# Cross attention with scores three steps in front, another order of VectorE's and ScalarE's work in a step, and the first scores inside the projection of V

## The chip, the cores and the metric

The kernel runs on one core of a Trainium2 chip. The metric is the device time of one execution in microseconds (us). Lower is better.

TensorE (PE in the profile) multiplies matrices and transposes; PEld is its loading of stationary operands. VectorE is DVE, ScalarE is ACT, GpSimd is POOL, and SyncE (SP) issues the loads of weights. Every engine works through its own list of instructions in order, and semaphores tie the lists together.

## The reference

Two transformer blocks on one sequence of 1024 tokens with width 1024. The change touches the cross attention of the first block alone: four heads of width 256 over a memory of 256 rows.

```
    xq = (rmsnorm(h, norm_x_g[l]) @ w_xq[l]).reshape(B, S, XATT_HEADS, XATT_HEAD_DIM)
    mn = rmsnorm(mem, norm_mem_g[l])
    xk = (mn @ w_xk[l]).reshape(B, M, XATT_HEADS, XATT_HEAD_DIM)
    xv = (mn @ w_xv[l]).reshape(B, M, XATT_HEADS, XATT_HEAD_DIM)
    sc = jnp.einsum('bshd,bmhd->bhsm', xq, xk).astype(jnp.float32) * (XATT_HEAD_DIM ** -0.5)
    pr = jax.nn.softmax(sc, axis=-1).astype(xv.dtype)
    xo = jnp.einsum('bhsm,bmhd->bshd', pr, xv).reshape(B, S, D_MODEL)
    h = h + xo @ w_xo[l]
```

## The kernel before

**Precision.** Every fp32 operand of a product is held as two parts, hi (rounded) and lo (the rest), and a product is three matmuls: hi by hi, hi by lo, lo by hi. ScalarE or GpSimd makes the hi part, and the lo part is a subtraction on VectorE or GpSimd.

**The stages around the change.** They follow each other in the lists of all engines, written out by hand:

1. Projection of K, eight jobs. SyncE loads a block of 512 KB into one of two slots of `raw`. GpSimd's `split` runs a tiny instruction (L524) and then makes `w_hi` (L525). VectorE's `memory_lo` makes `w_lo` (L2040), which also lets SyncE load the slot anew. TensorE multiplies (L657). ScalarE copies the result to `KTH` and VectorE subtracts to get `KTL` (L2053), which frees the PSUM slot.
2. Projection of V, eight blocks k. The same pipeline of weights, but all blocks are summed in the two PSUM slots `PJ[0]` and `PJ[1]` (L870). In between VectorE makes the lo parts of the queries with `query_low` (L2048), `B_lo` from `XQ` and `B_hi`, both in SBUF. In the end ScalarE makes `XVH` (L1404) and VectorE `XVL` (L2060), which frees the two slots.
3. The attention: 16 steps i, each for 128 tokens and two heads. In a step TensorE computes the scores (`x_score`, 12 matmuls, L888). VectorE takes the maxima of the two heads and scales them (`x_maximum`, L2065 and L2068). ScalarE takes the exponentials with their sums (`x_exp`, L1412). VectorE inverts the sums and scales the probabilities `XP` (`x_norm`, L2072 and L2074). TensorE transposes them (`x_turn`, L897). ScalarE copies the result to `XPT_hi` (`x_copy`, L1421), and VectorE subtracts to get `XPT_lo` (`x_split`, L2080). After four steps the transposed probabilities of 512 tokens are complete, and from then on each step also has one product with V (`x_values`, 6 matmuls, L909). ScalarE copies its result to `B_hi` (`x_out`, L1426), and VectorE subtracts to get `B_lo` (L2085).
4. The output projection, whose first job takes four of its eight blocks between the last value products (L657), and then the rest.

Before the change TensorE's iteration i is score(i+2), values(i-5), turn(i). VectorE's is out(i-6), split(i-1), maximum(i+2), norm(i+1). ScalarE's is out(i-6), copy(i-1), exp(i+2). All of `x_score(2)` and later waits for both PSUM slots to be free after the projection of V. A value product n waits for the `B_lo` of product n-2, since two PSUM banks take turns.

## Time and profile before

| what | value |
|---|---|
| median of three runs | 2959.33 us (2959.02 to 2960.76) |
| the profiled execution's own time | 2960.54 us |
| its span, first to last instruction | 2958.5 us |
| mean granted TensorE clock | 0.997 |
| TensorE matmuls busy | 2893.2 us, 98% of the span |
| VectorE busy | 1896.5 us, 64% |
| ScalarE busy | 1031.2 us, 35% |
| GpSimd busy | 1278.3 us, 43% |

The stages above lie between 570 and 707 us of the span. The shares are means over the whole kernel. The cross attention is under 4% of it, and TensorE's share there has to be read from its own stretch.

### The profile page before, as it was taken

How to read it: one execution, taken by the hardware profiler on the slowest of the kernel's cores; microseconds unless marked ns; L12 is line 12 of the kernel's file. 1: busy time of each engine (PE TensorE's matmuls, PEld its weight loads, DVE VectorE, ACT ScalarE, POOL GpSimd, SP SyncE). 2: the span in 40 equal slices, each digit the busy share in tenths (PEclk: the TensorE clock that was granted, in tenths of full speed). 3: DMA queues.
4: the chain of work that ended last, by engine and by line, in shares of the span. 5: the costliest groups of instructions: out<-in, count | busy, mean ns of one | idle time of the engine just before them, and what ended most of it. 6: DMA issues, size and time to landing. Idle time of an engine off the chain costs nothing.

```text
span 2958.5 us, 37245 instructions
## 1 busy us (share of the span) xinstructions
PE 2893.2 (98%) x14048; PEld 2336.6 (79%) x14048; DVE 1896.5 (64%) x1849; ACT 1031.2 (35%) x1411; POOL 1278.3 (43%) x1043
## 2 busy tenths in 40 slices
PE   9999999978999999999999999999999999999998
PEld 7887778867878888888777777888688778888886
DVE  7998764465575787776565656221675856778764
ACT  4116751133343332223253435112732533233321
POOL 0003323331364677763333332332433646777760
PEclk9999999999999999999999999999999999999999
DMA  3131021220132423232212121421431224232231
GB/s 143 50 74 49 2 97 46 78 79 21 36 110 100 154 94 108 98 107 86 114 61 79 60 76 59 163 105 50 181 142 46 86 97 143 98 123 100 100 114 57
DMA packets 77840, 265.29 MB, mean 90 GB/s; under 512 B 7552, under 2 KB 8064, under 8 KB 74368
## 3 DMA queue, kind: packets, MB, share of 16 engines
q1 hardware_dynamic: 57552, 183.89, 18.5%
q10 hardware_dynamic: 20144, 79.44, 7.4%
q8 instruction: 95, 1.56, 0.2%
q14 instruction: 49, 0.40, 0.0%
HBM read 208.25 MB, written 52.95 MB: 88 GB/s over the span
## 4 chain that ended last, share of the span: by engine, by line
PE 78%; DVE 11%; ACT 5%; DMA 4%; issue 2%; POOL 1%; ACTq 0%; DVEq 0%; SPq 0%; POOLq 0%
PE psum L657 50%; PE psum L947 15%; PE psum L1161 3%; DMA hid<-TT 2%; PE psum L1046 2%; PE psum L762 1%; DMA raw<-weights 1%; PE psum L778 1%; PE psum L792 1%; DVE WSX L2107 1%; ACT TT L1508 1%; DVE SX L2107 1%; DVE TT L2151 1%; PE psum L1112 1%; PE psum L1099 1%
## 5 line engine op out<-in xcount | busy, mean ns | idle before, releaser
L657 PE MATMUL psum<-A_hi,w_hi 128*128 128x512 f32 x1536 | 478.8, 393 | 1.7 <-POOL w_lo L536 0.5
L524 POOL TENSOR_TENSOR small<-par 128x1 f32<-128x1 f32 x149 | 42.3, 284 | 997.8 <-PE psum L657 844.0
L657 PE MATMUL psum<-A_lo,w_hi 128*128 128x512 f32 x1536 | 473.3, 389 | 0.0
L657 PE MATMUL psum<-A_hi,w_lo 128*128 128x512 f32 x1536 | 472.9, 389 | 0.0
L657 PEld LDWEIGHTS psum<-A_hi,w_hi 128*128 128x128 f32 x1536 | 287.0, 188 | 68.4 <-issue 6.9
L657 PEld LDWEIGHTS psum<-A_hi,w_lo 128*128 128x128 f32 x1536 | 288.3, 188 | 60.3
L657 PEld LDWEIGHTS psum<-A_lo,w_hi 128*128 128x128 f32 x1536 | 288.3, 188 | 60.2
L530 POOL TENSOR_TENSOR w_lo<-raw,w_hi 128x1024 fp32r<-128x1024 f32 (+1 forms) x133 | 331.0, 2488 | 11.1
L657 PE MATMUL psum<-B_hi,w_hi 128*128 128x512 f32 x832 | 257.5, 391 | 1.1 <-DVE B_lo L2319 1.1
L657 PE MATMUL psum<-B_hi,w_lo 128*128 128x512 f32 x832 | 256.1, 389 | 0.0
L657 PE MATMUL psum<-B_lo,w_hi 128*128 128x512 f32 x768 | 236.5, 389 | 0.0
L947 PE MATMUL psum<-XS,w_hi 128*128 128x512 f32 x768 | 236.3, 389 | 0.0
L947 PE MATMUL psum<-XS,W 128*128 128x512 f32 x864 | 211.8, 389 | 1.0 <-POOL w_lo L608 1.0
L947 PEld LDWEIGHTS psum<-XS,W 128*128 128x128 f32 x864 | 161.9, 188 | 35.6 <-POOL w_lo L608 2.2
L548 POOL TENSOR_SCALAR P<-P,small 128x704 f32<-128x704 f32 x64 | 54.5, 864 | 313.1 <-DVE small L1914 313.1
L657 PEld LDWEIGHTS psum<-B_hi,w_hi 128*128 128x128 f32 x832 | 156.0, 188 | 34.6 <-DVE B_lo L2319 1.5
L657 PEld LDWEIGHTS psum<-B_hi,w_lo 128*128 128x128 f32 x832 | 156.2, 188 | 32.5
L657 PEld LDWEIGHTS psum<-B_lo,w_hi 128*128 128x128 f32 x768 | 144.2, 188 | 30.0
L947 PEld LDWEIGHTS psum<-XS,w_hi 128*128 128x128 f32 x768 | 144.2, 188 | 29.8
L1463 ACT ACTIVATE XS<-XSF 128x1024 fp32r<-128x1024 f32 x84 | 89.3, 1063 | 223.7 <-DMA XSF<-hid 107.3
L998 PE MATMUL psum<-SX,WX_hi 128*128 128x512 f32 x512 | 158.3, 390 | 6.9 <-DVE SX L2107 6.9
L525 POOL TENSOR_SCALAR w_hi<-raw 128x1024 fp32r<-128x1024 f32 (+1 forms) x149 | 155.2, 1042 | 0.0
(361 smaller groups left out, 5522.2 us busy)
## 6 DMA issues: line engine op xcount, KB each, us to landing
raw<-weights SPq DMA_DIRECT2D x256, 512.0 KB, 3.3
hid<-TT ACTq DMA_DIRECT2D x60, 512.0 KB, 2.7
XSF<-hid SPq DMA_DIRECT2D x48, 512.0 KB, 5.3
BM<-rel_bias ACTq DMA_DIRECT2D x8, 1152.0 KB, 7.9
gate_spill<-RU SPq DMA_DIRECT2D x16, 512.0 KB, 3.0
ULF<-hid SPq DMA_DIRECT2D x6, 1024.0 KB, 7.0
x_spill<-H ACTq DMA_DIRECT2D x1, 4096.0 KB, 12.1
R<-gate_spill ACTq DMA_DIRECT2D x8, 512.0 KB, 4.6
```

The costliest lines, as they stand in the source:

```text
L524: pool.tensor_tensor(small[:, 12:13], par[:, 0:1], par[:, 0:1], ALU.mult)
L525: hi = pool.tensor_scalar(w_hi[:, s, 0:kb], raw[:, s, 0:kb], 1.0, 1.0, ALU.mult, ALU.mult)
L530: pool.tensor_tensor(w_lo[:, s, 0:kb], raw[:, s, 0:kb], f32(w_hi[:, s, 0:kb]), ALU.subtract).then_inc(S["w_split"], 1)
L548: pool.tensor_scalar(probs, probs, rsums[p % 3][:, h:h + 1], 1.0, ALU.mult, ALU.mult).then_inc(S["probs"], 1)
L657: last = pe.matmul(PJ[s][:, c:c + step], w[:, s, k, :], b[:, k, c:c + step], start=(k == 0 and i == 0), stop=(k == kblocks - 1 and i == 2))
L762: last = pe.matmul(pair_bank(p, h)[:, at_key:at_key + n], Q[rows, m, query:query + P], moving, start=True, stop=True)
L947: last = pe.matmul(bank, w[a][:, at_w + i, :], XS[layer][:, x, b, i, :], start=(i == 0 and t == 0), stop=(i == 1 and t == 2))
L998: last = pe.matmul(bank, WX[a][:, slot, k, :], moving[b][:, k, :], start=(k == 0 and i == 0), stop=(k == 3 and i == 2))
L1046: last = pe.matmul(PX[:, 1024 * g + HALF * h:1024 * g + HALF * h + HALF], WG[slot][:, 2 * d + g, :], RU[:, HALF * h:HALF * h + HALF], star ...
L1161: last = pe.matmul(fin_bank(n), w, x[:, k, half_of(h)], start=(k == 0 and i == 0), stop=(k == KB - 1 and i == 2))
L1463: tallies["st_hi"](act.activation(x[:, i, 0], xf[:, i, 1], ACT.Copy))
L2107: tally(dve.tensor_tensor(out, a, b, ALU.subtract))
```

## The change

It has five parts, all in the cross attention. No matmul, no load and no ScalarE instruction is added or removed.

- Scores 0 and 1 are computed inside the projection of V, behind its blocks 3 and 4. In the loop the score runs three steps in front, not two. The score banks are assigned so that step 2 needs only `PJ[0]` and step 4 only `PJ[1]`.
- TensorE's iteration becomes score(i+3), turn(i), values(i-5). The four early blocks of the output projection come one iteration earlier, and the last two value products follow each other.
- VectorE's iteration becomes maximum(i+3), norm(i+1), split(i-1), out(i-6). ScalarE's becomes copy(i-1), out(i-6), exp(i+3).
- The two scalings of the maxima (two instructions of one column) become one of two columns.
- The eight `query_low` are spread over the projections of K and V, at most one between two `memory_lo`. ScalarE's `XVH` of the first slot no longer waits for the second slot's last matmuls, and maxima, exponentials and norms of steps 0 and 1 stand in front of `XVL`.

```diff
         def x_bank(i):
-            at_col = 3072 + HALF * i if i < 2 else HALF * (i % 4)
+            at_col = 3072 + HALF * i if i < 2 else HALF * ((i - 2) % 4)
...
             def x_score(i):
                 pair, t = i // TT, i % TT
-                if i == 2:
-                    for s in range(2):
-                        pe.wait_ge(free[s], ROUNDS["xo"])
+                if i % TT == 0:
+                    pe.wait_ge(S["x_lo"], 4 * pair + 4)
+                if i in (2, 4):
+                    pe.wait_ge(free[i // 2 - 1], ROUNDS["xo"])
...
+            for k in range(KB):
+                q, s = ROUNDS["xv"] + k // 2, k % 2
+                wait_split(pe, q, s, "memory")
+                for r in range(2):
+                    if k == 0:
+                        pe.wait_ge(free[r], q)
...
+                    if k == KB - 1 and r == 0:
+                        last.then_inc(S["xv_half"], 1)
+                last.then_inc(S["products"], 1)
+                if k in (3, 4):
+                    x_score(k - 3)
...
-            x_score(0)
-            x_score(1)
-            for i in range(X_STEPS + X_BEHIND):
-                if i + 2 < X_STEPS:
-                    x_score(i + 2)
+            x_turn(0)
+            x_score(2)
+            x_turn(1)
+            x_score(3)
+            x_score(4)
+            for i in range(2, X_STEPS + X_BEHIND):
+                if i + 3 < X_STEPS:
+                    x_score(i + 3)
+                if i < X_STEPS:
+                    x_turn(i)
                 if i >= X_BEHIND:
                     x_values(i - X_BEHIND)
-                if i < X_STEPS:
-                    x_turn(i)
-                elif i < X_STEPS + 4:
-                    job(ROUNDS["xo"], 0, B, order=[i - X_STEPS], ready=outputs_ready)
+                if X_STEPS - 1 <= i < X_STEPS + 3:
+                    if i == X_STEPS - 1:
+                        pe.wait_ge(S["x_exp"], 2 * X_STEPS)
+                    job(ROUNDS["xo"], 0, B, order=[i - X_STEPS + 1], ready=outputs_ready)
...
             x_exp(0)
             x_exp(1)
-            for i in range(X_STEPS + X_BEHIND + 1):
+            act.wait_ge(S["xv_half"], 1)
+            tallies["m_hi"](act.activation(XVH[:, 0, :], PJ[0], ACT.Copy))
+            wait_job(act, ROUNDS["xv"] + 3, 1)
+            tallies["m_hi"](act.activation(XVH[:, 1, :], PJ[1], ACT.Copy))
+            x_copy(0)
+            x_exp(2)
+            x_copy(1)
+            x_exp(3)
+            x_exp(4)
+            for i in range(2, X_STEPS + X_BEHIND + 1):
+                if 2 < i <= X_STEPS:
+                    x_copy(i - 1)
                 if i > X_BEHIND:
                     x_out(i - X_BEHIND - 1)
-                if 1 <= i <= X_STEPS:
-                    x_copy(i - 1)
-                if i + 2 < X_STEPS:
-                    x_exp(i + 2)
+                if i + 3 < X_STEPS:
+                    x_exp(i + 3)
...
-                for block in {8: (0, 1), 9: (2, 3), 10: (4,), 11: (5,), 12: (6,), 13: (7,)}.get(n, ()):
-                    query_low(block)
+                if n in (1, 3, 5, 7, 8, 9, 10, 11):
+                    query_low(n // 2 if n < 8 else n - 4)
+                if n in (12, 13):
+                    x_maximum(n - 12)
+            x_norm(0)
+            x_norm(1)
             for r in range(2):
                 dve.wait_ge(S["m_hi"], 18 + r)
                 dve.tensor_tensor(XVL[:, r, :], PJ[r], f32(XVH[:, r, :]), ALU.subtract).then_inc(free[r], 4)
...
-                for e in range(2):
-                    done = tl["x_max"] if e else chain
-                    done(dve.tensor_scalar(lowest[e][i % 3], mx[:, e:e + 1], -X_DH ** -0.5, None, ALU.mult))
+                tl["x_max"](dve.tensor_scalar(lowest_of[i % 3], mx, -X_DH ** -0.5, None, ALU.mult))
...
-            for i in range(X_STEPS + X_BEHIND + 1):
-                if i > X_BEHIND:
-                    x_out(i - X_BEHIND - 1)
-                if 1 <= i <= X_STEPS:
-                    x_split(i - 1)
-                if i + 2 < X_STEPS:
-                    x_maximum(i + 2)
-                if i + 1 < X_STEPS:
-                    x_norm(i + 1)
+            x_split(0)
+            x_maximum(2)
+            x_split(1)
+            x_maximum(3)
+            x_norm(2)
+            x_maximum(4)
+            for i in range(2, X_STEPS + X_BEHIND + 1):
+                if i + 3 < X_STEPS:
+                    x_maximum(i + 3)
+                if 2 <= i < X_STEPS - 1:
+                    x_norm(i + 1)
+                if 2 < i <= X_STEPS:
+                    x_split(i - 1)
+                if i > X_BEHIND:
+                    x_out(i - X_BEHIND - 1)
```

The same three moves as the built programs have them. First VectorE in the projection of V, before the change: `w_lo` is `memory_lo`, `B_lo` is `query_low`, two of them behind one `w_lo` at first.

```order
458 L2040 TENSOR_TENSOR w_lo<-raw,w_hi 128x1024 x2
459 L2048 TENSOR_TENSOR B_lo<-XQ,B_hi 128x1024 x2
460 L2040 TENSOR_TENSOR w_lo<-raw,w_hi 128x1024
461 L2048 TENSOR_TENSOR B_lo<-XQ,B_hi 128x1024 x2
462 L2040 TENSOR_TENSOR w_lo<-raw,w_hi 128x1024
463 L2048 TENSOR_TENSOR B_lo<-XQ,B_hi 128x1024
```

The same engine after the change, from the last blocks of the projection of V to `XVL` and the first `split`.

```order
470 L2085 TENSOR_TENSOR B_lo<-XQ,B_hi 128x1024
471 L2054 TENSOR_TENSOR w_lo<-raw,w_hi 128x1024
472 L2062 TENSOR_REDUCE small<-psum 128x2
473 L2063 TENSOR_SCALAR small<-small 128x2
474 L2054 TENSOR_TENSOR w_lo<-raw,w_hi 128x1024
475 L2062 TENSOR_REDUCE small<-psum 128x2
476 L2063 TENSOR_SCALAR small<-small 128x2
477 L2067 RECIPROCAL small<-small 128x2
478 L2069 TENSOR_TENSOR XP_105<-XP_105,small 128x512
479 L2067 RECIPROCAL small<-small 128x2
480 L2069 TENSOR_TENSOR XP_106<-XP_106,small 128x512
481 L2101 TENSOR_TENSOR XVL<-psum,XVH 128x1024 x2
```

The maxima of steps 0 and 1 moved in between and behind the last `w_lo`, and two norms now stand in front of the two `XVL`, for which scores 2 and 4 wait.

Next, one iteration of VectorE in the middle of the attention, before the change (XP_105 to XP_108 are the four buffers of probabilities, the first B_lo and XPT_lo are out and split).

```order
512 L2085 TENSOR_TENSOR B_lo<-psum,B_hi 128x512
513 L2080 TENSOR_TENSOR XPT_lo_112<-psum,XPT_hi_110 128x4x128
514 L2065 TENSOR_REDUCE small<-psum 128x2
515 L2068 TENSOR_SCALAR small<-small 128x1 x2
516 L2072 RECIPROCAL small<-small 128x2
517 L2074 TENSOR_TENSOR XP_105<-XP_105,small 128x512
```

And after it.

```order
517 L2062 TENSOR_REDUCE small<-psum 128x2
518 L2063 TENSOR_SCALAR small<-small 128x2
519 L2067 RECIPROCAL small<-small 128x2
520 L2069 TENSOR_TENSOR XP_105<-XP_105,small 128x512
521 L2075 TENSOR_TENSOR XPT_lo_112<-psum,XPT_hi_110 128x4x128
522 L2080 TENSOR_TENSOR B_lo<-psum,B_hi 128x512
```

The maximum went from behind out and split to their front, and lost one of its two scalings.

Last, ScalarE in the middle of the attention before the change: exp (XP), out (B_hi), copy (XPT_hi).

```order
321 L1412 ACTIVATE XP_106,small<-psum,small 128x256 x2
322 L1426 ACTIVATE B_hi<-psum 128x512
323 L1421 ACTIVATE XPT_hi_110<-psum 128x4x128
324 L1412 ACTIVATE XP_107,small<-psum,small 128x256 x2
325 L1426 ACTIVATE B_hi<-psum 128x512
```

And after it.

```order
320 L1417 ACTIVATE XP_106,small<-psum,small 128x256 x2
321 L1426 ACTIVATE XPT_hi_110<-psum 128x4x128
322 L1431 ACTIVATE B_hi<-psum 128x512
323 L1417 ACTIVATE XP_107,small<-psum,small 128x256 x2
324 L1426 ACTIVATE XPT_hi_109<-psum 128x4x128
```

Copy and out changed places, and the exponentials between them are those of a step one further in front.

## Rows read from the trace of the kernel before

**Rows 1.** The waits from 595 to 707 us: us in total, times, longest.

```profile
PE psum L897 <- DVE XP L2074: 14.7, 14, 2.7
PE psum L870 <- DVE w_lo L2040: 4.4, 5, 1.5
```

**Rows 2.** Stretches: length, PE, PEld, DVE, ACT, POOL busy, granted clock, DMA share, GB/s.

```profile
632.00:635.00 3.00, 3.00 (x17) 3.00 (x17) 1.80 (x6) 1.73 (x5) 0.00 (x0) 0.57 0.00 0
...
660.00:683.00 23.00, 17.72 (x111) 14.35 (x110) 16.68 (x36) 11.65 (x30) 0.00 (x0) 1.00 0.00 1
```

**Rows 3.** TensorE in order of time: start, us, instruction, idle before it.

```profile
595.53 0.70 PE L870 MATMUL psum<-w_hi,MH 128*128 128x512 f32 x2 [1.09 <-DVE KTL L2053]
...
605.65 0.74 PE L870 MATMUL psum<-w_hi,MH 128*128 128x512 f32 x2 [1.52 <-DVE w_lo L2040]
...
613.57 0.72 PE L870 MATMUL psum<-w_hi,MH 128*128 128x512 f32 x2 [0.37 <-DVE w_lo L2040]
...
620.63 0.73 PE L870 MATMUL psum<-w_hi,MH 128*128 128x512 f32 x2 [0.52 <-DVE w_lo L2040]
...
627.40 0.36 PE L888 MATMUL psum<-KTH,B_hi 128*128 128x256 f32 x1 [0.89 <-DVE XVL L2060]
...
631.81 1.11 PE L897 MATMUL psum<-ident,XP 128*128 128x128 f32 x4 [2.74 <-DVE XP L2074]
...
647.46 0.40 PE L909 MATMUL psum<-XPT_hi,XVH 128*128 128x512 f32 x1
...
682.55 0.50 PE L909 MATMUL psum<-XPT_hi,XVH 128*128 128x512 f32 x1 [0.39 <-DVE XPT_lo L2080]
...
706.98 0.62 PE L657 MATMUL psum<-B_hi,w_hi 128*128 128x512 f32 x2
```

**Rows 4.** TensorE in one step: turn, first score, first value matmul.

```profile
657.58 0.66 PE L897 MATMUL psum<-ident,XP 128*128 128x128 f32 x4 [1.03 <-DVE XP L2074]
658.00 0.36 PE L888 MATMUL psum<-KTH,B_hi 128*128 128x256 f32 x1
...
659.50 0.40 PE L909 MATMUL psum<-XPT_hi,XVH 128*128 128x512 f32 x1
```

**Rows 5.** VectorE in the same step.

```profile
658.58 0.69 DVE L2085 TENSOR_TENSOR B_lo<-psum,B_hi 128x512 fp32r<-128x512 f32 x1 [1.05 <-ACT B_hi L1426]
659.30 0.69 DVE L2080 TENSOR_TENSOR XPT_lo<-psum,XPT_hi 128x512 fp32r<-128x512 f32 x1
660.03 0.69 DVE L2065 TENSOR_REDUCE small<-psum 128x2 f32<-128x512 f32 x1
660.76 0.34 DVE L2068 TENSOR_SCALAR small<-small 128x1 f32<-128x1 f32 x2
661.13 0.17 DVE L2072 RECIPROCAL small<-small 128x2 f32<-128x2 f32 x1
661.33 0.69 DVE L2074 TENSOR_TENSOR XP<-XP,small 128x512 f32<-128x512 f32 x1
```

**Rows 6.** ScalarE from one step's exponentials to the next.

```profile
656.68 0.47 ACT L1412 ACTIVATE XP<-psum,small 128x256 f32<-128x256 f32 x1 [2.07 <-DVE small L2068]
...
657.88 0.60 ACT L1426 ACTIVATE B_hi<-psum 128x512 fp32r<-128x512 f32 x1
...
661.18 0.47 ACT L1412 ACTIVATE XP<-psum,small 128x256 f32<-128x256 f32 x1 [2.08 <-DVE small L2068]
```

**Rows 7.** VectorE and GpSimd side by side in the projection of V and behind it.

```profile
600.98 3.36 DVE L2048 TENSOR_TENSOR B_lo<-XQ,B_hi 128x1024 fp32r<-128x1024 f32 x2
602.22 1.05 POOL L525 TENSOR_SCALAR w_hi<-raw 128x1024 fp32r<-128x1024 f32 x1
...
622.86 2.41 POOL L530 TENSOR_TENSOR w_lo<-raw,w_hi 128x1024 fp32r<-128x1024 f32 x1
624.90 2.36 DVE L2060 TENSOR_TENSOR XVL<-psum,XVH 128x1024 fp32r<-128x1024 f32 x2 [3.19 <-ACT XVH L1404]
```

More of the change, by code:

```diff
@@ L195, in build @@
         sums = [small[:, 82 + 2 * i:84 + 2 * i] for i in range(3)]
+        lowest_of = [small[:, 76 + 2 * i:78 + 2 * i] for i in range(3)]
         rsums = [small[:, 88 + 2 * i:90 + 2 * i] for i in range(3)]
@@ L859, in _ @@
             rounds("xk", 4, (MH, ML), width=N_MEM)
-            for k in range(KB):
-                q, s = ROUNDS["xv"] + k // 2, k % 2
-                wait_split(pe, q, s, "memory")
-                if k == 0:
-                    for slot in range(2):
-                        pe.wait_ge(free[slot], q)
-                for r in range(2):
-                    for a, b in ((MH, w_hi), (ML, w_hi), (MH, w_lo)):
-                        wide = b[:, s].rearrange("p a b -> p (a b)")
-                        for c in range(2):
-                            last = pe.matmul(PJ[r][:, HALF * c:HALF * c + HALF], a[:, k, P * r:P * r + P],
-                                             wide[:, HALF * c:HALF * c + HALF],
-                                             start=(k == 0 and b is w_hi and a is MH), stop=(k == KB - 1 and b is w_lo))
-                last.then_inc(S["products"], 1)
-            split_by[0] = "late"
             def x_score(i):
                 pair, t = i // TT, i % TT
-                if i == 2:
-                    for s in range(2):
-                        pe.wait_ge(free[s], ROUNDS["xo"])
+                if i % TT == 0:
+                    pe.wait_ge(S["x_lo"], 4 * pair + 4)
+                if i in (2, 4):
+                    pe.wait_ge(free[i // 2 - 1], ROUNDS["xo"])
                 if i >= 6:
@@ L890, in x_score @@
                 last.then_inc(S["x_scores"], 1)
+            for k in range(KB):
[4 more added lines that the diff above has]
+                        pe.wait_ge(free[r], q)
+                    for a, b in ((MH, w_hi), (ML, w_hi), (MH, w_lo)):
+                        wide = b[:, s].rearrange("p a b -> p (a b)")
+                        for c in range(2):
+                            last = pe.matmul(PJ[r][:, HALF * c:HALF * c + HALF], a[:, k, P * r:P * r + P],
+                                             wide[:, HALF * c:HALF * c + HALF],
+                                             start=(k == 0 and b is w_hi and a is MH), stop=(k == KB - 1 and b is w_lo))
+                    if k == KB - 1 and r == 0:
[3 more added lines that the diff above has]
+                    x_score(k - 3)
+            split_by[0] = "late"
             def x_turn(i):
@@ L911, in x_values @@
                 last.then_inc(S["x_pv"], 1)
[L913 to L918 removed]
+            outputs_ready = (S["x_lo"], [KB + 8 * (k // 4) + 5 + k % 4 for k in range(KB)])
+            x_turn(0)
[8 more added lines that the diff above has]
+                    x_turn(i)
                 if i >= X_BEHIND:
                     x_values(i - X_BEHIND)
[L921 to L924 removed]
+                if X_STEPS - 1 <= i < X_STEPS + 3:
+                    if i == X_STEPS - 1:
+                        pe.wait_ge(S["x_exp"], 2 * X_STEPS)
+                    job(ROUNDS["xo"], 0, B, order=[i - X_STEPS + 1], ready=outputs_ready)
             job(ROUNDS["xo"], 0, B, order=[4, 5, 6, 7], ready=outputs_ready)
@@ L1401, in _ @@
                 tallies["m_hi"](act.activation(B_hi[:, n, :], XQ[:, n, :], ACT.Copy))
-            wait_job(act, ROUNDS["xv"] + 3, 1)
-            for r in range(2):
-                tallies["m_hi"](act.activation(XVH[:, r, :], PJ[r], ACT.Copy))
             def x_exp(i):
@@ L2044, in _ @@
                 memory_lo(ROUNDS["xk"], s)
-            def query_low(n):
-                dve.wait_ge(S["m_hi"], 2 * n + 3)
-                chain(dve.tensor_tensor(B_lo[:, n, :], XQ[:, n, :], f32(B_hi[:, n, :]), ALU.subtract))
-            for n in range(2 * KB):
-                if n < KB:
-                    dve.wait_ge(S["m_hi"], 2 * n + 2)
-                    dve.tensor_tensor(KTL[:, n, :], PJ[n % 2][:, 0:N_MEM], f32(KTH[:, n, :]), ALU.subtract).then_inc(free[n % 2], 1)
-                if n + 2 < 2 * KB:
-                    memory_lo(ROUNDS["xk"] + 1 + n // 2, n % 2)
-                for block in {8: (0, 1), 9: (2, 3), 10: (4,), 11: (5,), 12: (6,), 13: (7,)}.get(n, ()):
-                    query_low(block)
-            for r in range(2):
-                dve.wait_ge(S["m_hi"], 18 + r)
-                dve.tensor_tensor(XVL[:, r, :], PJ[r], f32(XVH[:, r, :]), ALU.subtract).then_inc(free[r], 4)
             def x_maximum(i):
```

19 lines of the change are left out of this document (14 added, 5 removed).

## The prediction

> **What bounds the kernel now.** I read the page first: TensorE's matmuls are busy 98% of the span, so a gain can only come where TensorE waits. Next I read who waited for whom from 595 to 707 us [rows 1]. TensorE's transposes waited 14.7 us, in 14 places, for VectorE's scaling of the probabilities. Its blocks in the projection of V waited 4.4 us for the lo parts of the weights. So this stretch is not bound by TensorE. Third, the stretch from 660 to 683 us, steps of the middle [rows 2]: TensorE is busy 17.72 of 23 us, VectorE 16.68, and the clock is fully granted. No engine is full, which is the mark of a ring: engines that hand one step's work around and wait for each other.
>
> The ring can be read from one step. ScalarE starts the exponentials at 656.68 and again at 661.18, 4.50 us later [rows 6]. They take 1.20 (656.68 to 657.88), and out copies 0.60 more [rows 6]. VectorE, after a hop of 0.1, does out and split (658.58 to 660.03, 1.45) and then the maximum with two scalings (660.03 to 661.10, 1.07) [rows 5], and a hop of 0.08 later the next exponentials begin. 1.20 + 0.60 + 0.10 + 1.45 + 1.07 + 0.08 = 4.50. The maximum stands behind out and split, which stand behind ScalarE's out, which stands behind the previous exponentials. TensorE is not in the ring. Its step is 0.42 of turn, 1.50 of scores [rows 4] and some 1.40 of values (six matmuls at 0.23), 3.32 together, so it idles 1.2 us in every 4.5.
>
> **The steady steps.** The change puts the maximum in front, so it waits only for a score made long ago. Following the new lists around: exp(i+3) feeds norm(i+3), which VectorE reaches two iterations later. Turn(i) waits for norm(i) and split(i-2) of the iteration before. Copy(i-1) and out(i-6) need only products of the iteration before. The longest ring left spans two iterations: VectorE's last out, a value product 1.4, a score 1.5 and 0.15 of hops, 3.1 us, while VectorE's own iteration in between takes longer. What remains is each engine's load. VectorE: maximum 0.73 + one scaling, norm 0.90, split 0.72, out 0.73 [rows 5]. A scaling of two columns isn't in the trace. It lies between half of the pair's 0.34 and the whole; I take 0.20 with its gap, as the reciprocal of two columns (0.17) does. Sum 3.29. ScalarE: 1.20 + 0.60 + 0.60 with gaps, 2.5 [rows 6]. TensorE 3.32. So a step costs 3.32 instead of 4.50, set by TensorE with VectorE just under it.
>
> **The projection of V.** Before, block 0 starts at 595.53 and blocks 1 and 2 follow densely, to 601.1. Blocks 3 and 4 each wait 1.52 for their `w_lo`, which stands behind two `query_low`. From block 5 on the period is 3.53 (613.57 to 620.63, two blocks), with one `query_low` in each [rows 3]. That period is the reload of a slot plus GpSimd's and VectorE's work in turn: while GpSimd makes `w_hi` (602.22), the second `B_lo` is held, so two of 1.22 take 3.36 [rows 7]. After the change every block has at most one `query_low`. The four that moved into the projection of K push the lo parts there back by 0.5 us. Against that, block 0 no longer waits 1.09 for the last `KTL`: its first half needs only slot 0, and it starts near 595.4. Laid end to end, block 2 starts at 601.5 and block 7 five periods of 3.55 later at 619.2. Its 2.85 end the projection at 622.1. The two scores, 1.45 each, lie in the 0.8 us per block that TensorE waits anyway, and are made up by block 7. Before, the projection and these two scores ended at 626.4. That is 4.3 gained.
>
> **Behind it a new stall.** TensorE does turn(0) and then needs `XVL` of slot 0. Maximum 0 ends at 617.0, behind the seventh `w_lo`. ScalarE loads its table (1.28) and has the first exponentials at 619.6. Norm 0 follows maximum 1 and ends at 621.6. Norm 1 reads `XP` and the inverted sums, both in SBUF, while GpSimd makes the lo part of the first block of the output projection, 2.41 long [rows 7], now from 621.55. I take it that it is held until 624.0, as the second `B_lo` was. `XVL` itself, which reads PSUM, ran at 1.2 next to that same GpSimd instruction [rows 7], so it isn't held. But it is queued behind the norm, 624.6 to 625.8, and score 2 starts there. Before, it started at 627.40 [rows 3]. The Trainium skill states the same in "SBUF — State Buffer", Who interferes with whom: a VectorE instruction with two SBUF inputs and a GpSimd instruction that reads SBUF exclude each other. The rows on `B_lo` and `XVL` agree with it.
>
> From 625.8 VectorE is dense: two `XVL` (from 624.6) 2.3, four splits 2.9, six maxima 5.6, four norms 3.7, and 1.9 of waiting for the exponentials and copy of steps 1 and 2. That is 16.4, to 641.0. The first value product, which needs split 3, starts at 641.6. I add the clock. Before, the 2.74 us wait at 631.81 [rows 3] was followed by a stretch at a granted clock of 0.57 for 3 us [rows 2], which costs 3 x 0.43 = 1.3. A stall of 3.2 us after turn(0) brings the same again. 642.9, against 647.46 [rows 3].
>
> **The sum.** Value product 8 comes eight steps later: 642.9 + 8 x 3.32 = 669.5, against 682.55 [rows 3]. From there to the fifth block of the output projection (706.98 before [rows 3]) TensorE has eight value products at 1.4, four blocks at 1.36 and three turns, 17.8. Before, this took 24.4. After, VectorE still works 2.3 a step for three steps, 0.7 more: 18.5, so 688.0. Back-to-back value products 14 and 15 add nothing, since the lo part of product 13 (1.5 after its end) is hidden by the 1.36 block and product 14. From 706.98 on TensorE was dense, and it stays so: the last `B_lo` comes 1.6 after product 15, behind three blocks (4.1). GpSimd's weights for the output projection are done by 628. All that follows moves rigidly. The gain is 706.98 - 688.0 = **19.0 us**: 4.6 up to the first value product, 8.5 in the eight steps, 5.9 in the tail. The same laying-out on the order of before gives 706.1 for the row at 706.98, so its error is about one. The profiled execution took 2960.54, which gives 2941.5. The median lies 1.2 under that execution: **2940.3 us**. This forecast, with a gain of 16 to 23, has 0.74; its own range is 2936.5 to 2943.5. At its lower end the norms are not held by GpSimd (2.2 more) and the clock does not dip (1.3 more).
>
> **Rivals.**
> 1. The lists are too evenly loaded. VectorE at 3.29 and TensorE at 3.32 wait for each other, or a scaling of two columns costs the full 0.34. If a step takes 3.9, then eleven steps give back 0.6 each: gain 12.4, 2947 us. For it: the hops of 0.1 on each handing over. Against it: every handing over has most of an iteration of slack. 0.16.
> 2. The ring isn't broken, because a dependency that I overlooked ties the new maximum to the same step's exponentials. Steps stay near 4.5 and only what comes before the first value product is gained, 4.6: 2954.7 us. For it: ScalarE's exponentials still follow out and copy. Against it: these no longer wait for anything of their own iteration. 0.06.
> 3. Slower: TensorE's clock stays at the lower of its levels, 1.2 GHz, behind the longer stall in front of score 2. At half clock a dense step takes 6.6 instead of 3.32. Each such step costs 3.3, so that six steps eat the gain and all sixteen make the kernel 34 us slower, 2993. For it: the new stall (3.2) is longer than the one (2.74) that brought the low clock. Against it: before, the clock was full again after 3 us and stayed so with TensorE idle a quarter of each step [rows 2]. 0.04.
>
> **How the numbers follow.** The measurement tells 0.2%, 5.9 us, from no change. Faster by more than that: the forecast and rival 1, 0.74 + 0.16 = 0.90, and nearly nothing of rival 2. Within 0.2%: rival 2, 0.06. Slower: 0.04. The range leaves out rivals 2 and 3 and the worse part of rival 1, and reaches from the forecast's lower end to 2947.5.
>
> **What the new profile would show.** TensorE's transposes waiting for `XP` falls from 14.7 us to 3 or 4. From step 5 on turns stand 3.3 apart, and VectorE is busy over 95% there. In the projection of V the waits for `w_lo` stay near 0.8 per block or vanish behind the scores. Between turn 0 and score 2 a wait of about 3 us for `XVL`, with a norm in front of it that lasts far over 0.69. After it possibly a stretch at a clock near 0.6. I am wrong if the steps stand 3.8 or more apart, if the stall before score 2 exceeds 6 us, or if TensorE begins to wait in the output projection.

## The result

The changed kernel takes 2941.78 us (median of four runs, 2940.80 to 2942.52), against 2959.60 us (2959.02 to 2960.76) before. The ratio is 0.9938, with a 95% interval of 0.9927 to 0.9950. That is 17.8 us less. Its profiled execution took 2941.72 us, with a span of 2939.5 us, 19.0 less than the 2958.5 of before. The forecast was 2940.3.

The profile after the change, read in the same order as before. First the waits from 590 to 692 us (us in total, times, longest), which answer to [rows 1].

```profile
PE psum L873 <- DVE XVL L2101: 2.9, 1, 2.9
...
PE psum L901 <- DVE XPT_lo L2075: 2.1, 3, 1.0
...
PE psum L901 <- DVE XP L2069: 1.6, 2, 0.8
...
PE psum L886 <- DVE w_lo L2054: 1.0, 2, 0.5
```

The transposes' wait for `XP`, 14.7 us in 14 places, has shrunk to 1.6 in 2, and the blocks' wait for `w_lo` from 4.4 to 1.0. Two new waits stand there: 2.9 us before score 2 for `XVL`, and 2.1 for the lo part of turned probabilities.

Then the stretches (length, PE, PEld, DVE, ACT, POOL busy, granted clock, DMA share, GB/s), which answer to [rows 2].

```profile
622.00:625.00 3.00, 0.18 (x1) 0.19 (x2) 2.91 (x3) 1.22 (x2) 2.92 (x4) 1.00 0.24 72
625.00:628.00 3.00, 3.00 (x27) 3.00 (x27) 2.35 (x4) 0.39 (x2) 1.99 (x1) 1.00 0.25 102
...
641.00:667.00 26.00, 24.95 (x165) 22.29 (x163) 23.38 (x46) 18.65 (x49) 0.00 (x0) 1.00 0.00 1
```

TensorE stands still from 622 to 625 while VectorE and GpSimd are both busy. Behind that the clock stays at 1.00: the stretch at 0.57 of [rows 2] has no counterpart. In the middle TensorE is busy 24.95 of 26 us, where it was busy 17.72 of 23.

TensorE's landmarks in order of time (start, us, instruction, idle before it), which answer to [rows 3]: first block of V, turn 0, score 2, value products 0 and 8, fifth block of the output projection.

```profile
594.60 0.73 PE L886 MATMUL psum<-w_hi,MH 128*128 128x512 f32 x2
...
621.34 0.60 PE L901 MATMUL psum<-ident,XP 128*128 128x128 f32 x4
...
624.82 0.39 PE L873 MATMUL psum<-KTH,B_hi 128*128 128x256 f32 x1 [2.88 <-DVE XVL L2101]
...
640.53 0.47 PE L913 MATMUL psum<-XPT_hi,XVH 128*128 128x512 f32 x1
...
666.97 0.47 PE L913 MATMUL psum<-XPT_hi,XVH 128*128 128x512 f32 x1
...
685.42 0.62 PE L658 MATMUL psum<-B_hi,w_hi 128*128 128x512 f32 x2
```

VectorE in one step of the middle, which answers to [rows 5]: maximum, scaling, inverse, norm, split, out, next maximum.

```profile
647.02 0.69 DVE L2062 TENSOR_REDUCE small<-psum 128x2 f32<-128x512 f32 x1
647.74 0.17 DVE L2063 TENSOR_SCALAR small<-small 128x2 f32<-128x2 f32 x1
647.95 0.17 DVE L2067 RECIPROCAL small<-small 128x2 f32<-128x2 f32 x1
648.15 0.69 DVE L2069 TENSOR_TENSOR XP<-XP,small 128x512 f32<-128x512 f32 x1
648.87 0.69 DVE L2075 TENSOR_TENSOR XPT_lo<-psum,XPT_hi 128x512 fp32r<-128x512 f32 x1
649.60 0.69 DVE L2080 TENSOR_TENSOR B_lo<-psum,B_hi 128x512 fp32r<-128x512 f32 x1
650.32 0.69 DVE L2062 TENSOR_REDUCE small<-psum 128x2 f32<-128x512 f32 x1
```

The step is 650.32 - 647.02 = 3.30 us, with nothing between the rows but some 0.03 each. ScalarE, which answers to [rows 6], now waits 0.89 us for a scaling, where it waited 2.07.

```profile
661.22 0.48 ACT L1417 ACTIVATE XP<-psum,small 128x256 f32<-128x256 f32 x1 [0.89 <-DVE small L2063]
```

Last VectorE and GpSimd side by side in front of score 2, which answer to [rows 7]: the two norms and the two `XVL`, and the `w_hi` and `w_lo` beside the norms.

```profile
619.45 1.22 DVE L2069 TENSOR_TENSOR XP<-XP,small 128x512 f32<-128x512 f32 x1
620.71 0.17 DVE L2067 RECIPROCAL small<-small 128x2 f32<-128x2 f32 x1
620.91 2.54 DVE L2069 TENSOR_TENSOR XP<-XP,small 128x512 f32<-128x512 f32 x1
623.54 2.36 DVE L2101 TENSOR_TENSOR XVL<-psum,XVH 128x1024 fp32r<-128x1024 f32 x2
...
619.09 1.05 POOL L526 TENSOR_SCALAR w_hi<-raw 128x1024 fp32r<-128x1024 f32 x1
620.22 2.68 POOL L531 TENSOR_TENSOR w_lo<-raw,w_hi 128x1024 fp32r<-128x1024 f32 x1
```

The first norm takes 1.22 and the second 2.54 instead of 0.69. Each ends some 0.5 us behind the GpSimd instruction beside it (620.67 and 620.14, 623.45 and 622.90). `XVL`, which reads PSUM, takes its usual 1.2 each.

### The profile page after: what moved, and what is told of

Read it like the earlier page. It is cut to its first block, busy times and chain, and to the rows that moved or that the text cites. A ratio compares the mean times of both kernels' runs of the same rounds, so it can differ in the third digit from the quotient of the medians.

```text
span 2939.5 us, 37231 instructions
## 1 busy us (share of the span) xinstructions
PE 2889.6 (98%) x14048; PEld 2337.0 (80%) x14048; DVE 1893.8 (64%) x1833; ACT 1031.4 (35%) x1411; POOL 1278.7 (44%) x1043
## 4 chain that ended last, share of the span: by engine, by line
PE 79%; DVE 11%; ACT 4%; DMA 3%; POOL 1%; issue 1%; ACTq 0%; DVEq 0%; SPq 0%; POOLq 0%
PE psum L658 50%; PE psum L956 16%; PE psum L1170 3%; DMA hid<-TT 2%; PE psum L1055 2%; PE psum L763 1%; PE psum L779 1%; PE psum L793 1%; DVE WSX L2125 1%; DMA raw<-weights 1%; ACT TT L1522 1%; DVE SX L2125 1%; DVE TT L2169 1%; PE psum L1121 1%; PE psum L1108 1%
```

## The experiments

Two theories stood at the start. A: the order of the lists breaks the ring of 4.50 us, and the rest of the gain comes from the scores inside the projection of V. B: the third step in front is what does it, since it gives every wait a step more of slack. Later runs ask what the new stall consists of, and what the other parts are worth.

All landmarks are counted from the first matmul of the projection of K (570.32 before, 569.93 after), since nothing in front of it is changed. "Turn 0" is the first transpose, "value 0" and "value 8" are the first matmuls of these value products, and "block 4" is the fifth block of the output projection, behind the last value product. "Step" is the distance of two maxima in the steady steps, which also have a value product. "Clock lost" is the sum of (1 - granted clock) x length over stretches of 2 us from 560 to 712. It is time at the lower clock, in us of full clock, and not what the kernel loses by it, since TensorE does not set the pace everywhere. All landmarks come from one profiled execution of each kernel.

| kernel | median us | ratio, interval | turn 0 | value 0 | value 8 | block 4 | step | clock lost |
|---|---|---|---|---|---|---|---|---|
| before | 2959.60 | | 61.49 | 77.14 | 112.23 | 135.30 | 4.50 | 1.7 |
| after | 2941.78 | 0.9938 (0.9927-0.9950) | 51.41 | 70.60 | 97.04 | 115.49 | 3.30 | 0 |
| order_only | 2947.37 | 0.9958 (0.9944-0.9971) | 61.48 | 77.01 | 104.64 | 124.29 | 3.48 | 3.4 |
| three_only | 2956.60 | 0.9992 (0.9983-1.0001) | 61.54 | 77.13 | 112.10 | 133.71 | 4.50 | 6.8 |
| merge_only | 2956.91 | 0.9994 (0.9985-1.0003) | 62.40 | 77.23 | 110.71 | 133.45 | 4.32 | 1.7 |
| query_spread | 2957.23 | 0.9993 (0.9984-1.0002) | 59.86 | 75.15 | 110.21 | 133.30 | 4.50 | 1.7 |
| order_and_merge | 2946.29 | 0.9953 (0.9940-0.9967) | 61.97 | 76.02 | 102.45 | 121.92 | 3.30 | 1.7 |
| scores_behind | 2947.49 | 0.9960 (0.9946-0.9973) | 57.81 | 77.35 | 103.73 | 122.20 | 3.30 | 3.4 |
| behind_two_scalings | 2949.80 | 0.9968 (0.9956-0.9980) | 57.21 | 77.80 | 105.42 | 123.88 | 3.48 | 3.4 |
| two_scalings | 2942.79 | 0.9945 (0.9932-0.9959) | 51.40 | 72.01 | 99.63 | 118.10 | 3.48 | 1.7 |
| norm1_behind | 2940.83 | 0.9938 (0.9925-0.9952) | 53.22 | 73.31 | 99.72 | 118.15 | 3.30 | 0 |
| split_after_norms | 2938.79 | 0.9932 (0.9919-0.9946) | 51.52 | 68.83 | 95.25 | 113.72 | 3.30 | 0 |
| copy1_first | 2941.31 | 0.9939 (0.9925-0.9953) | 51.69 | 70.76 | 97.19 | 115.63 | 3.30 | 1.7 |
| both | 2939.14 | 0.9930 (0.9917-0.9944) | 51.23 | 68.46 | 94.89 | 113.36 | 3.30 | 0 |

The intervals of three_only, merge_only and query_spread reach over 1, so their medians alone tell no gain; they are read by their landmarks.

### The parts, each put into the kernel before

**order_only**: the new order inside an iteration, two steps in front as before.

```diff
                 if i + 2 < X_STEPS:
                     x_score(i + 2)
-                if i >= X_BEHIND:
-                    x_values(i - X_BEHIND)
                 if i < X_STEPS:
                     x_turn(i)
+                if i >= X_BEHIND:
+                    x_values(i - X_BEHIND)
...
-                if i > X_BEHIND:
-                    x_out(i - X_BEHIND - 1)
-                if 1 <= i <= X_STEPS:
-                    x_split(i - 1)
                 if i + 2 < X_STEPS:
                     x_maximum(i + 2)
                 if i + 1 < X_STEPS:
                     x_norm(i + 1)
+                if 1 <= i <= X_STEPS:
+                    x_split(i - 1)
+                if i > X_BEHIND:
+                    x_out(i - X_BEHIND - 1)
```

> The kernel before with one edit: in the loop of the attention VectorE takes maximum(i+2), norm(i+1), split(i-1), out(i-6), ScalarE copy before out, TensorE turn before values. Scores stay two steps in front, the projection of V is untouched. Theory A (a ring through out, split, maximum and the exponentials set the 4.5 us of a step, and the order opens it): steps of 3.3 to 3.5 us, set by VectorE's own 3.47, and 11 to 13 us less than before, more than half of the whole change. Theory B (it is the third step in front that hides the chain): steps stay near 4.5 and under 3 us are gained.

Measured: the step falls from 4.50 to 3.48, and block 4 comes 11.0 us earlier, nearly all of it behind value product 0 (77.01 against 77.14): 7.5 up to value product 8 and 3.4 in the tail. The median is 12.1 lower, as expected.

**three_only**: the third step in front alone.

```diff
+            x_score(2)
             for i in range(X_STEPS + X_BEHIND):
-                if i + 2 < X_STEPS:
-                    x_score(i + 2)
+                if i + 3 < X_STEPS:
+                    x_score(i + 3)
```

> The kernel before with scores, maxima and exponentials three steps in front, and the order within a step left as it was. Theory A: the ring is closed as before, steps stay at 4.5, and 0 to 2 us are gained (only at the end, where the last steps have no score). Theory B: 10 us or more are gained.

Measured: the step stays at 4.50. The stretch from 655 to 675 us of this kernel and of order_only:

```profile
655.00:675.00 20.00, 15.15 (x94) 12.11 (x93) 14.42 (x33) 10.51 (x29) 0.00 (x0) 1.00 0.00 1
```

```profile
655.00:675.00 20.00, 20.00 (x130) 17.46 (x129) 18.70 (x39) 13.77 (x36) 0.00 (x0) 1.00 0.00 1
```

With three steps in front VectorE still works only 14.42 of 20 us, the mark of the ring; with the order alone it works 18.70. Theory B is refuted, and A stands. Block 4 comes 1.6 us earlier, in the tail, which takes 21.6 instead of 23.1. This execution had the lower clock twice, from 638 to 645 and from 682 to 690 us, which may hide some of the gain at both ends. It doesn't touch the steps between them: they stand 4.50 apart at full clock.

**merge_only**: one scaling of two columns in place of two of one.

```diff
-                for e in range(2):
-                    done = tl["x_max"] if e else chain
-                    done(dve.tensor_scalar(lowest[e][i % 3], mx[:, e:e + 1], -X_DH ** -0.5, None, ALU.mult))
+                tl["x_max"](dve.tensor_scalar(lowest_of[i % 3], mx, -X_DH ** -0.5, None, ALU.mult))
```

> The kernel before with the two scalings of the maxima made one of two columns. Theory A: both scalings lie in the ring, so a step falls by the 0.19 us that VectorE saves, from 4.50 to 4.31, and 2 to 3 us are gained over 14 steps. If no ring is closed there (theory B, where the chain's length is hidden or not as a whole), a gain of 0 to 1 us.

Measured: the step is 4.32, so the scaling lies in the old ring with its full 0.17; the stretch from value 0 to value 8 gets 35.09 - 33.48 = 1.6 us shorter. The first scaling showed something else. VectorE, and GpSimd's `w_lo` beside it:

```profile
629.21 1.02 DVE L2067 TENSOR_SCALAR small<-small 128x2 f32<-128x2 f32 x1
...
627.82 2.38 POOL L531 TENSOR_TENSOR w_lo<-raw,w_hi 128x1024 fp32r<-128x1024 f32 x1
```

It took 1.02 us instead of 0.17, and ended 0.03 after GpSimd (630.23 against 630.20).

**query_spread**: the eight `query_low` at most one between two `memory_lo`.

```diff
-                for block in {8: (0, 1), 9: (2, 3), 10: (4,), 11: (5,), 12: (6,), 13: (7,)}.get(n, ()):
-                    query_low(block)
+                if n in (1, 3, 5, 7, 8, 9, 10, 11):
+                    query_low(n // 2 if n < 8 else n - 4)
```

> The kernel before with the eight query_low spread over the projections of K and V, at most one between two lo parts of weights. Expected: the two waits of 1.5 us of TensorE in the projection of V shrink to about 0.5, the projection ends 2 to 2.6 us earlier, and all of it is kept, since the attention behind it starts that much earlier: 2 to 2.6 us gained. The rival: what moved into the projection of K delays the weights there by as much, and nothing is gained.

Measured: TensorE's wait for `w_lo` in the projection of V falls from 4.4 to 2.2 us, value product 0 comes 2.0 earlier, at the lower end of what was expected, and nothing behind it changes.

**order_and_merge**: order_only with merge_only's edit.

> The kernel before with two parts of the change: the new order of the lists and the one scaling of two columns, but scores still two steps in front and nothing moved into the projection of V. It asks what the third step in front is worth once the order is new. Theory A (with the new order every engine is limited by its own load, VectorE's above all): a step takes 3.30 to 3.32 as in the changed kernel, so that the third step is worth nothing in the middle; the region takes 2.5 to 3 us less than with the order alone (16 steps by 0.17); median near 2945.5. Theory B (with two in front a ring is left: exponentials, norm, turn within one iteration): the step stays near 3.48, because a shorter VectorE only waits longer; region and median as with the order alone, 2947.4.

Measured: the step is 3.30, exactly as with three steps in front, and the eight steps from value 0 to value 8 take 26.43 (after: 26.44). In the middle the third step in front is worth nothing. The second scaling's 0.17 is in the step (3.48 against 3.30) wherever it is taken out or put in: VectorE's list sets the pace. TensorE is close behind it. From the start of its last transpose to the start of the first value matmul it takes 0.25 to 0.27 us at a step of 3.48 and 0.07 to 0.10 at 3.30, so it has under 0.1 us left, and a still shorter list of VectorE would gain little more. The first scaling is held here too: it took 1.01 (from 626.98, beside a `w_lo` that ended at 627.97). The median fell by only 1.1 against order_only and the intervals overlap; the landmarks carry the reading.

### What the early scores are worth

**scores_behind**: the changed kernel with scores, maxima 0 and 1 behind the projection of V.

```diff
-                if k in (3, 4):
-                    x_score(k - 3)
             split_by[0] = "late"
+            x_score(0)
+            x_score(1)
...
-                if n in (12, 13):
-                    x_maximum(n - 12)
+            x_maximum(0)
+            x_maximum(1)
             x_norm(0)
```

> The changed kernel with scores 0 and 1 (and their maxima) put back behind the projection of V, all else kept. Theory: they then cost their 2.9 us in full, their table load and first exponentials no longer lie under the projection, and the kernel takes 4 to 5 us more than the changed one, so 14 to 16 less than before. Rival: the wait in front of score 2 shrinks by as much as the scores cost, since the norms then start after GpSimd's split, and under 2 us are lost.

Measured: block 4 comes 6.7 us later than in the changed kernel, more than expected. TensorE waits 3.56 us before turn 0 and 1.96 before score 2, the clock drops, and both scalings are held. VectorE, then GpSimd:

```profile
623.24 0.66 DVE L2063 TENSOR_SCALAR small<-small 128x2 f32<-128x2 f32 x1
624.02 0.69 DVE L2062 TENSOR_REDUCE small<-psum 128x2 f32<-128x512 f32 x1
624.74 1.57 DVE L2063 TENSOR_SCALAR small<-small 128x2 f32<-128x2 f32 x1
...
622.82 1.05 POOL L526 TENSOR_SCALAR w_hi<-raw 128x1024 fp32r<-128x1024 f32 x1
623.96 2.34 POOL L531 TENSOR_TENSOR w_lo<-raw,w_hi 128x1024 fp32r<-128x1024 f32 x1
```

**behind_two_scalings**: the same with two scalings of one column each.

```diff
-                tl["x_max"](dve.tensor_scalar(lowest_of[i % 3], mx, -X_DH ** -0.5, None, ALU.mult))
+                for e in range(2):
+                    done = tl["x_max"] if e else chain
+                    done(dve.tensor_scalar(lowest[e][i % 3], mx[:, e:e + 1], -X_DH ** -0.5, None, ALU.mult))
```

> Scores 0 and 1 behind the projection of V, as in the run of that name, but with the two scalings of one column in place of the one of two columns. In that run the scalings of two columns beside GpSimd's instructions took 0.66 and 1.57 us where 0.17 is normal. Theory (a scaling of two columns is held by GpSimd like the norm, one of one column is not): each pair takes 0.34 there, turn 0 comes 1.2 to 1.9 us earlier than the 57.8 us behind the start of the projection of K that it took, and the steps are 3.49 long instead of 3.30, so that over the eight steps to value product 8 about 1.4 us are lost again. Rival (the long scalings come from something else that reads or writes there at that time, whatever the form): the pairs take 0.8 to 1.7 us as well and turn 0 comes no earlier.

Measured, VectorE at the same place, and GpSimd beside it:

```profile
623.26 0.34 DVE L2065 TENSOR_SCALAR small<-small 128x1 f32<-128x1 f32 x2
...
624.77 0.34 DVE L2065 TENSOR_SCALAR small<-small 128x1 f32<-128x1 f32 x2
...
622.83 1.05 POOL L526 TENSOR_SCALAR w_hi<-raw 128x1024 fp32r<-128x1024 f32 x1
623.96 2.34 POOL L531 TENSOR_TENSOR w_lo<-raw,w_hi 128x1024 fp32r<-128x1024 f32 x1
```

GpSimd's rows stand at the same times, and the pairs take 0.34: the form of the scaling decides. Turn 0 came only 0.6 us earlier, not 1.2 to 1.9, because norm 0 now waits 1.13 us for its exponentials where it waited 0.21; the held scaling had mostly covered that wait. The whole is 1.7 slower at block 4: 1.2 of it in the eight longer steps, and the rest nearly all in front of value product 0.

**two_scalings**: the changed kernel with that same edit.

> The changed kernel with two scalings of one column again. Theory: VectorE's own work sets the pace of the steps then, 3.47 us against TensorE's 3.30, so a step takes 3.5 and the kernel 2 to 2.5 us more than the changed one. Rival (TensorE sets the pace and VectorE has slack): under 0.5 us.

Measured: steps of 3.48, and block 4 is 2.6 us later: 1.2 between value 0 and value 8, and 1.4 in front of value 0. In that first part the clock was low for a while too (0.73 from 624 to 626 us and 0.50 from 626 to 628), behind a wait of 2.67: maximum 2 starts 2.41 us behind the first matmul of score 2, where it started 1.81 behind it. So about 0.6 of the 2.6 goes with the clock, and some 2.0 are the price of the scalings. The median is only 1.0 higher, and the intervals overlap.

### What the stall in front of score 2 consists of

**norm1_behind**: norm 1 between the two `XVL`, so that the first `XVL` and score 2 don't wait for it.

```diff
             x_norm(0)
-            x_norm(1)
             for r in range(2):
                 dve.wait_ge(S["m_hi"], 18 + r)
                 dve.tensor_tensor(XVL[:, r, :], PJ[r], f32(XVH[:, r, :]), ALU.subtract).then_inc(free[r], 4)
+                if r == 0:
+                    x_norm(1)
```

> The changed kernel with the norm of step 1 put between the two XVL instead of in front of both. Theory (the norm is held by GpSimd's instruction, and XVL of slot 0 only queues behind it): score 2 starts about 2 us earlier, the wait of 2.9 us in front of it falls to about 1, the norm still lasts over 0.69 us, and 1 to 1.5 us are kept at the end, since VectorE sets the pace right behind. Rival (XVL comes late by itself, from ScalarE's XVH): score 2 starts when it does now, nothing is gained.

Measured: a miss. Block 4 is 2.7 us later in the profiled execution, and the median (2940.83) is not told apart from the changed kernel's. VectorE in order, then GpSimd:

```profile
619.02 1.03 DVE L2063 TENSOR_SCALAR small<-small 128x2 f32<-128x2 f32 x1
620.09 0.17 DVE L2067 RECIPROCAL small<-small 128x2 f32<-128x2 f32 x1
620.29 2.74 DVE L2069 TENSOR_TENSOR XP<-XP,small 128x512 f32<-128x512 f32 x1
...
624.45 2.65 DVE L2069 TENSOR_TENSOR XP<-XP,small 128x512 f32<-128x512 f32 x1
...
618.98 1.04 POOL L526 TENSOR_SCALAR w_hi<-raw 128x1024 fp32r<-128x1024 f32 x1
620.11 2.37 POOL L531 TENSOR_TENSOR w_lo<-raw,w_hi 128x1024 fp32r<-128x1024 f32 x1
```

Here the scaling starts at 619.02, 0.04 behind GpSimd's `w_hi`, and is held. After the change it started at 619.05, 0.04 ahead of `w_hi` (619.09), and took 0.17:

```profile
619.05 0.17 DVE L2063 TENSOR_SCALAR small<-small 128x2 f32<-128x2 f32 x1
```

From there the norms fall against `w_lo` differently: both are held for over 2.6. Such an order is decided by less than 0.1 us, so this run says little about the place of norm 1. Its expectation had treated the meeting as fixed.

**split_after_norms**: GpSimd begins its work for the output projection only behind norms 0 and 1.

```diff
+            pool.wait_ge(S["x_probs"], 2)
             splits(ROUNDS["xo"], ROUNDS["ff"])
```

> The changed kernel with GpSimd waiting for the norms of steps 0 and 1 before it starts on the weights of the output projection. Theory (VectorE's norm with two operands in SBUF and GpSimd's instruction exclude each other): both norms last 0.69 us instead of 1.22 and 2.54, score 2 starts about 2 us earlier, and about 2 us are gained over the changed kernel. If the long norms have another cause they stay long and nothing is gained.

Measured: every norm takes 0.69. TensorE before score 2:

```profile
622.65 0.39 PE L874 MATMUL psum<-KTH,B_hi 128*128 128x256 f32 x1 [1.00 <-DVE XVL L2102]
```

The wait is 1.00 instead of 2.88, block 4 comes 1.8 us earlier, and all five runs (2938.24 to 2940.64) lie below all four of the changed kernel, though the two ratios' intervals overlap. GpSimd was the cause of the stall's larger part, and its delay costs nothing: from 680 to 900 us TensorE waits for the same things as after the change (4.0 us in total against 3.9).

### Two attempts at more

**copy1_first**: ScalarE's copy 1 before exponentials 2.

```diff
             x_copy(0)
-            x_exp(2)
             x_copy(1)
+            x_exp(2)
```

> The changed kernel with two entries of ScalarE's list exchanged: the copy of step 1 stands in front of the exponentials of step 2. In the changed kernel VectorE idles behind the maximum of step 2 until the split of step 1, which waits for that copy, which stands behind the 1.2 us of exponentials. Theory (between the stall and the first value product VectorE's list sets the pace, not the number of operations but who waits for whom): that idle time shrinks by some 1.2 us and reappears only in part, since norm 2 then waits for its exponentials; the first value product comes 1.2 to 1.7 us earlier, and the region up to the fifth block of the output projection (index 4) takes 1.5 us less than in the changed kernel; median 2940.3. Rival (TensorE's own list or the clock sets that stretch): nothing moves, region within 0.3 us of the changed kernel.

Measured: block 4 stays (115.63 against 115.49), as the rival said, and for one of the two reasons that it names, the clock. TensorE waited 2.85 us before score 2, as before the edit, and this time the clock fell. Score matmuls behind the stall, and the two maxima that wait for the scores:

```profile
628.19 0.41 PE L873 MATMUL psum<-KTL,B_hi 128*128 128x256 f32 x1
628.40 0.41 PE L873 MATMUL psum<-KTH,B_lo 128*128 128x256 f32 x1
...
627.43 0.69 DVE L2062 TENSOR_REDUCE small<-psum 128x2 f32<-128x512 f32 x1 [0.39 <-PE psum L873]
630.59 0.69 DVE L2062 TENSOR_REDUCE small<-psum 128x2 f32<-128x512 f32 x1 [0.93 <-PE psum L873]
```

The matmuls follow each other every 0.21 us instead of 0.12. The same work, from the tenth matmul of score 2 to the tenth of score 3, took 3.35 us (626.55 to 629.90) against 1.88 after the change (625.99 to 627.87). VectorE waits 0.39 and 0.93 us there for scores for which it did not wait after the change. Without these waits the exchange might have shown 1.3 to 1.5; that is an estimate, not a run, and the exchange has not been seen alone at full clock.

**both**: this exchange and GpSimd's wait together.

> The changed kernel with the exchange in ScalarE's list and with GpSimd's split for the output projection waiting for norms 0 and 1. If the two edits remove waits that follow each other on VectorE, their gains add up only in part, because with norm 1 out of the way the exponentials of step 2 end earlier as well: the region takes 2.7 us less than in the changed kernel, 0.9 less than with GpSimd waiting alone; median 2939. If they are independent, 1.8 + 1.5 = 3.3 us less. If GpSimd's later weights were late for the output projection (rival), TensorE would wait in front of its first block and nothing would be gained over the version in which GpSimd waits alone.

Measured: block 4 is 0.4 us earlier than with GpSimd's wait alone, not 0.9, and 0.3 of that lies in front of turn 0, where the two kernels have the same instructions. The medians (2939.14 and 2938.79) are not told apart. So the exchange gave nothing that can be seen. The clock stayed full. VectorE's scaling of step 3, and GpSimd beside it:

```profile
627.15 1.81 DVE L2064 TENSOR_SCALAR small<-small 128x2 f32<-128x2 f32 x1
...
626.53 2.40 POOL L531 TENSOR_TENSOR w_lo<-raw,w_hi 128x1024 fp32r<-128x1024 f32 x1
```

The exchange moved a scaling of two columns beside `w_lo`, and it was held for 1.6 us, all but 0.1 of what the exchange had freed (with GpSimd's wait alone split 1 starts at 627.35, here at 625.68). The two versions with GpSimd's wait are the fastest of the study; split_after_norms is the simpler one.

## Why the prediction was right

**The steady steps: right.** Forecast 3.32, measured 3.30, and 26.44 us for eight steps against 26.56. That the ring was broken by the order is shown by order_only and three_only. One half sentence was the wrong way round: TensorE was said to set the step, with VectorE just under it. VectorE has no wait in the steady steps, and its 0.17 appears in the step; TensorE has under 0.1 us left. TensorE's transposes wait 1.6 us for `XP` in all, where 3 or 4 were forecast. "VectorE busy over 95%" was said a little too high: 3.10 us of instructions in 3.30 are 94% by the rows.

**The projection of V: right.** It was said to end at 622.1; turn 0 stands at 621.34 (0.4 of the difference is an earlier start of the whole). Two of its blocks wait, 0.5 each. That the spread `query_low` shortens these waits is shown by query_spread.

**The stall before score 2: right in kind and near in size.** Said: norm 1 held, score 2 at 625.8. Measured: 624.82, with norm 1 at 2.54. GpSimd's `w_lo` began at 620.22, not 621.55, so the norm was released at 623.45, not 624.0. The Trainium skill's rule in "SBUF — State Buffer", Who interferes with whom, which the prediction used, is now tested by taking GpSimd away (split_after_norms). The first norm was held as well, 0.5 over the normal, and that was not foreseen.

**The clock: wrong.** 1.3 us were put in for a stretch at the lower level behind the stall, since one had followed a wait of 2.74 before. It did not come after 2.88. It came after 2.85 (copy1_first) and 2.67 (two_scalings). So the length of a wait of this size does not tell whether TensorE falls to 1.2 GHz. The term should have been a range from 0 up to the 1.5 by which the same work took longer in copy1_first, not a number. Value product 0 was forecast at 642.9 and came at 640.53: 1.3 of the 2.4 is this term, 1.0 the earlier score 2.

**The tail: a misread row.** The prediction took 706.98 for the fifth block of the output projection before the change. The trace of the kernel before, from the last value matmul on:

```profile
705.39 0.39 PE L909 MATMUL psum<-XPT_hi,XVL 128*128 128x512 f32 x1
705.62 0.62 PE L657 MATMUL psum<-B_hi,w_hi 128*128 128x512 f32 x2
706.07 0.62 PE L657 MATMUL psum<-B_lo,w_hi 128*128 128x512 f32 x2
706.52 0.61 PE L657 MATMUL psum<-B_hi,w_lo 128*128 128x512 f32 x2
706.98 0.62 PE L657 MATMUL psum<-B_hi,w_hi 128*128 128x512 f32 x2
```

The fifth block begins at 705.62, right behind the last value matmul, and has six matmuls; 706.98 is the sixth block. So the tail took 23.07 before, not 24.4. After the change it took 18.45, as forecast (18.5), and gave 4.6, not 5.9. The prediction had a sign of it: its laying-out of the order of before gave 706.1 for the fifth block, which is 0.9 from the row that it took and 0.5 from the right one.

**The sum: its parts right within 2.3 us, and the total nearer than that by luck.** Forecast 4.6 + 8.5 + 5.9 = 19.0. Measured at block 4: 6.9 + 8.65 + 4.6 = 20.2 (0.4 of it because the whole stretch began earlier). The clock term and the early score 2 made the first part 2.3 too small, and the misread row made the last 1.3 too large. The span gained 19.0 nonetheless, since from block 4 to the end the changed kernel took 1.2 us more (2254.1 against 2252.9), where its instructions are the same. Over all fourteen kernels that rest lies between 2251.5 and 2254.1, with no relation to the edits; what makes it scatter is not known. It bounds what a single profiled execution can tell, and effects under some 1.5 us of the median are left open here.

**The parts.** From before to after block 4 moves by 135.30 - 115.49 = 19.8. The order gives 11.0 and the merged scaling 2.4 on top (order_and_merge, part of it a shorter time at the low clock). The remaining 6.4 come with the other parts together. Taking the early scores out of the changed kernel costs 6.7 (in an execution that also lost 3.4 us at the lower clock, which the changed one did not), and leaves it level with order_and_merge (122.20 and 121.92). So the early scores are needed for these 6.4, with the spread `query_low` that make room for them (2.0 alone). How the 6.4 divide between them and the clock is not shown: scores_behind reaches turn 0 4.2 us before order_and_merge but value 0 1.3 us after it, so the two differ by more than the early scores. The third step in front has no measured worth in the middle. In the tail it has some: three_only, which changes nothing else, takes 1.5 less there than the kernel before. With the new order the changed kernel is 1.0 faster in the tail than order_and_merge (18.45 against 19.47). Its early output blocks may have a part in this; they were not run apart.

## What to carry to other kernels

When no engine is full, write down one step's waits as a ring before asking for more depth: a new order of three engines' lists, with the maximum that starts the next exponentials at the front of VectorE's, took 1.0 us off a step, and one step more of lookahead took off nothing. Which of the three lists did it was not run apart. Instructions that can hold each other (here VectorE's with GpSimd's) belong at times that a wait keeps apart, since otherwise edits elsewhere shift who comes first by 0.1 us and cost or give 1 to 2 us. And check each landmark row by its neighbours: the row before and behind it tells which block it is.

## What the runs showed of the hardware

**A scaling of two columns is held by GpSimd, one of one column is not.** Normal is 0.15 to 0.17 for either. Beside GpSimd's `w_hi` or `w_lo` the form 128x2 took 0.66, 1.01, 1.02, 1.03, 1.57 and 1.81 in six places of five kernels (scores_behind, order_and_merge, merge_only, norm1_behind, both), and each time it ended 0.02 to 0.03 us behind GpSimd's instruction. The form 128x1 took 0.34 a pair at the very places of 0.66 and 1.57. The inverse of two columns is not held either: the one at 620.71 after the change stands inside `w_lo` and took 0.17. The Trainium skill has what would explain the scalings, in "VectorE: DVE Perf Modes", Mode 2×_2P: an instruction with one tensor input, with source and destination in SBUF, can read it through both ports when its outermost dimension other than 1 is even. The Trainium skill's "SBUF — State Buffer", Who interferes with whom, has tensor_scalar among the instructions that then contend with GpSimd. The rows on the scalings agree with that; the prediction took only the rule on two inputs from it.

**Equal waits, different clocks.** TensorE's idle time of 2.88 us left the granted clock at 1.00, while 2.85 and 2.67 at the same place were each followed by 1.7 us lost at the lower level. In front of turn 0 a wait of 2.74 was followed by 1.7 lost in the kernel before and by 3.4 in order_only. In norm1_behind waits of 1.6, 0.66, 1.07 and 2.40 were followed by none, but in three_only the clock fell at 638 us behind waits of 1.3 and 1.93. Nothing in the rows read here tells these cases apart.
